# The beginning of a decoder trunk on one core: norm weights ahead of unit 0, later units requested behind its landing, and transposes by diagonal products and by pairs

## The reference, cut to what matters

```python
def rmsnorm(x, g):
    y = xf * lax.rsqrt(jnp.mean(xf * xf, axis=-1, keepdims=True) + EPS)
    return (y * g.astype(jnp.float32)).astype(x.dtype)
...
    a_u, a_v, b_q, b_k, b_v, c_b, c_c, c_x, d_a, d_g = split_cols(h @ w_in)
    y_a = sgu_mixer(a_u, a_v, ...)          # gelu of a_u and a_v first
```

## Time and profile before

| what | value |
|---|---|
| median of 3 runs | 771.77 us (771.01 to 772.01) |
| the profiled execution's own time | 771.82 us |
| its span, first to last instruction | 768.9 us |
| mean granted TensorE clock | 0.999 |
| busy: PE, PEld | 757.4 us (98%), 679.2 us (88%) |
| busy: DVE, ACT, POOL | 637.1 us (83%), 499.6 us (65%), 22.5 us (3%) |
| line 914, DVE, w_lo of a full unit | mean 2195 ns, x140 |
| line 564, ACT, w_hi of a full unit | mean 1841 ns, x140 |
| chain that ended last | PE 95%, DVE 2%, ACT 1%, issue 1%, DMA 1% |

### The profile page before, as it was taken

How to read it: one execution, slowest core, us unless ns; L and a number is a source line. 1 busy time by engine, 2 the same in 40 slices (tenths; PEclk the granted TensorE clock), 3 DMA queues, 4 the chain that set the end, 5 groups by cost and what they waited for, 6 DMA issues and landing times.

```text
span 768.9 us, 12945 instructions
## 1 busy us (share of the span) xinstructions
PE 757.4 (98%) x4794; PEld 679.2 (88%) x4794; DVE 637.1 (83%) x856; ACT 499.6 (65%) x592; POOL 22.5 (3%) x42
## 2 busy tenths in 40 slices
PE   7999999999999999999999999999999999999997
PEld 7899999999878888888799999999988888888885
DVE  5858899469779998989785779956977999898995
ACT  7535566645588877777662547565548978776773
POOL 4030000000000000000001000000000000000000
PEclk9999999999999999999999999999999999999999
DMA  8866345357727999999465553534764599999961
GB/s 306 280 220 218 112 165 165 100 197 253 257 72 270 327 388 347 354 344 333 139 219 166 189 194 113 189 111 139 271 215 170 175 346 356 367 355 331 346 240 55
DMA packets 86418, 180.57 MB, mean 235 GB/s; under 512 B 13238, under 2 KB 25176, under 8 KB 86360
## 3 DMA queue, kind: packets, MB, share of 16 engines
q1 hardware_dynamic: 86360, 179.79, 67.2%
HBM read 178.72 MB, written 1.05 MB: 234 GB/s over the span
## 4 chain that ended last, share of the span: by engine, by line
PE 95%; DVE 2%; ACT 1%; issue 1%; DMA 1%; POOL 0%; DVEq 0%; ACTq 0%; POOLq 0%
PE bank L1507 28%; PE bank L1509 28%; PE bank L1508 28%; PE bank L1913 2%; PE bank L1824 1%; PE bank L1794 1%; PE bank L1939 1%; PE bank L1673 1%; PE bank L1578 1%; DMA x<-in_x 1%; PE bank L1581 0%; PE bank L1787 0%; ACT gates L574 0%; ACT gates L587 0%; PE bank L1908 0%
## 5 line engine op out<-in xcount | busy, mean ns | idle before, releaser
L914 DVE TENSOR_TENSOR w_lo<-raw,w_hi 128x2048 fp32r<-128x2048 f32 (+1 forms) x140 | 304.7, 2195 | 54.8 <-ACT w_hi L564 54.0
L564 ACT ACTIVATE w_hi<-raw 128x2048 fp32r<-128x2048 f32 (+1 forms) x140 | 256.1, 1841 | 127.6 <-PE bank L1509 126.9
L1507 PE MATMUL bank<-a_hi,w_hi 128*128 128x256 f32 x688 | 195.8, 285 | 0.6 <-DVE a_lo L980 0.6
L1509 PE MATMUL bank<-a_lo,w_hi 128*128 128x256 f32 x688 | 194.6, 283 | 0.0
L1508 PE MATMUL bank<-a_hi,w_lo 128*128 128x256 f32 x688 | 194.6, 283 | 0.0
L1507 PE MATMUL bank<-w_hi,y_lo 128*128 128x512 f32 x408 | 161.2, 395 | 0.0
L1509 PE MATMUL bank<-w_lo,y_lo 128*128 128x512 f32 x408 | 159.2, 390 | 0.0
L1507 PEld LDWEIGHTS bank<-a_hi,w_hi 128*128 128x128 f32 x688 | 131.9, 192 | 1.6 <-issue 1.5
L1508 PEld LDWEIGHTS bank<-a_hi,w_lo 128*128 128x128 f32 x688 | 132.0, 192 | 0.1
L1509 PEld LDWEIGHTS bank<-a_lo,w_hi 128*128 128x128 f32 x688 | 132.0, 192 | 0.0
L1508 PE MATMUL bank<-w_hi,y_hi 128*128 128x512 f32 x272 | 106.1, 390 | 0.0
(11 more groups left out here) (334 smaller groups left out, 960.8 us busy)
## 6 DMA issues: line engine op xcount, KB each, us to landing
raw<-in_w_gate SPq DMA_DIRECT2D x56, 512.0 KB, 4.6
raw<-in_w_e_gate SPq DMA_DIRECT2D x42, 512.0 KB, 4.5
raw<-in_w_e_up SPq DMA_DIRECT2D x42, 512.0 KB, 6.1
mid<-in_w_e_down SPq DMA_DIRECT2D x36, 512.0 KB, 5.9
raw<-in_w_in SPq DMA_DIRECT2D x32, 512.0 KB, 6.2
raw<-in_w_e_gate SPq DMA_DIRECT2D x40, 256.0 KB, 4.6
raw<-in_w_e_up SPq DMA_DIRECT2D x40, 256.0 KB, 5.6
mid<-in_w_e_down SPq DMA_DIRECT2D x40, 256.0 KB, 5.4
```

The lines of the kernel that those rows point to most:

```text
L564: a.activation(w_hi[:, at.part(n), 0:w], raw_at(slot)[:, 0:w], ACT.Copy).then_inc(hi_done, at.count(n))
L914: v.tensor_tensor(w_lo[:, part, 0:w], raw_at(slot)[:, 0:w], w_hi[:, part, 0:w].bitcast(F32), ALU.subtract).then_inc(split_done, at.count(n))
L1507: mm(ps, a2[0], b2[0], start=first, stop=False, skip_group_check=shared)
L1509: return mm(ps, a2[0], b2[1], start=False, stop=last, skip_group_check=shared)
```

## The change

- SyncE issues the norm weights of layer 0 ahead of unit 0. Behind unit 0 it waits until both its DMAs have landed, and only then requests units 1 to 3 and all that stands behind them.
- Layer 0, half 0: DVE copies x unscaled into tile order when it has landed, and scales the identity matrix by the row factors (a diagonal matrix). TensorE multiplies each tile by the diagonal, which transposes and scales at once. Half 1: DVE scales all eight tiles, ScalarE none; TensorE transposes them as before.
- Layer 0: h_hi of k = 0 and 1 is made by DVE, directly ahead of their h_lo, instead of by ScalarE, whose high part of unit 0 no longer stands behind a scaling. The semaphore of h_hi is raised by 3 at k = 2 to make up for them.
- `keep_warm` goes from 14 to 11 products ahead of the transposes and from 6 to 4 behind, in layer 0.
- Layer 1: TensorE waits for both scaled halves and then transposes by pairs: tiles k and k + 4 of both halves (four transposes), then the signal for that pair. Before, half 1's transposes gave the signals.

```diff
+            norm_gains(0)
             load(At(0, 0, False), 0, *units_a[0], 0)
-            norm_gains(0)
+            sp.wait_ge(landed[0], 16 * DMAS)
             first_units(At(0, 0, False), 0, 1)
...
-            scale_part(0)
             hi(At(0, 0, False), 0)
...
-                for k in range(KT):
+                for k in range(0 if l else 2, KT):
...
+                if l == 0:
+                    dve.wait_ge(pool_consts, 3)
+                    dve.wait_ge(x_loaded[0], 16)
+                    v.tensor_copy(xn[:, 0, :, :], x[:, 0, :].rearrange("q (p c) -> q c p", c=KT)).then_inc(S("n1_x"), 1)
+                    mean_square_in(0)
+                    dve.wait_ge(S("n1_rs"), 1)
+                    v.tensor_scalar(diag[:, 0, :], ident[:, :], rs1[:, 0:1], None, ALU.mult).then_inc(S("n1_d"), 1)
+                    mean_square_in(1)
+                    scaled(1, 0)
...
+                    if l == 0 and k < 2:
+                        dve.wait_ge(par_g, 16)
+                        dve.wait_ge(S("n1_t"), k + 1)
+                        v.tensor_scalar(h_hi[:, k, :], bank[4 + k][:, 0:256], g1[:, k:k + 1], None,
+                                        ALU.mult).then_inc(S("h_hi_first"), 1)
+                        dve.wait_ge(S("h_hi_first"), k + 1)
...
-                keep_warm(4, 16 if l else 14)
...
+                keep_warm(4, 16 if l else 11)
...
+                    for k in range(KT):
+                        mm(turned_at(0, k), xn[:, 0, k, :], diag[:, 0, :], start=True, stop=True, skip_group_check=True)
+                    pe.wait_ge(S("n1_x"), T)
+                    for k in range(4):
+                        tp(turned_at(1, k), xn[:, 1, k, :], ident[:, :])
+                        tp(turned_at(1, k + 4), xn[:, 1, k + 4, :], ident[:, :]).then_inc(S("n1_t"), 1)
+                    keep_warm(3, 4)
+                else:
+                    pe.wait_ge(S("n1_x"), T * (l + 1))
+                    pe.wait_ge(S("n1_xa"), l)
+                    for k in range(4):
+                        for kk in (k, k + 4):
+                            for t in range(T):
+                                last = tp(turned_at(t, kk), xn[:, t, kk, :], ident[:, :])
+                        last.then_inc(S("n1_t"), 1)
```

## The result

The changed kernel takes 773.73 us (median of 15 executions, 770.85 to 777.34), the kernel before beside it 771.62 us (median of 15, 770.51 to 772.99). The ratio is 1.0029, with a 95% interval of 1.0018 to 1.0041: slower by 0.3%. The forecast was 771.9 with a range up to 773.6, and "the same" as the likeliest case.

A forecast was written before the change was run, and what follows sets the result against it. TensorE alone was taken to bound nearly everything after the first product. The 1.75 us front gain was eaten by later requests (0.2 us slower), layer 1 cost 0: span 769.1, time 771.9 us, range 769.9 to 773.6.

The forecast's parts named there:

- the compute chain: Layer 0, ahead of the first weight product: it starts 1.75 us earlier, at 11.25 to 11.4 instead of 13.10.
- a bound of 1.3: Layer 0's diagonal products: hidden at the fast pace, cost 0; at 0.213 us each they delay half 1 by 1.3 us.
- Landings: SyncE's queue at the start: unit 0 landed at 8.95, unit 1 at 14.3, unit 3 at 19.8 instead of 16.9.
- my own sign (8.8 to 9.1): Unit 0's landing: the forecast would be wrong if it came at another time than 8.8 to 9.1.
- layer 1: Layer 1's transposes by pairs: cost 0, from -0.1 to +0.3 us.
- The delay d: SyncE's request of unit 4: 2.9 us later, at 24.6 for 21.67; 0.7 to 5.6 possible.
- case B: SyncE regains its holding in issuing: d 0.7 to 2.6, front gain partly or wholly through, 770.0 to 770.8; chance 0.28.
- case A: The forecast: landings pace SyncE, d 2.6 to 3.3, net 0.15 us faster to 0.6 slower, 771.6 to 772.4; chance 0.5.
- The limit that I summed at: TensorE at unit 4, 2.74 us in hand: net gain the smaller of 1.75 and 2.74 - d, giving -0.2 us.
- The stall: TensorE waiting for layer 0's mixer parameters: landed near 24, TensorE there at 22.9, about 1 us.
- The step that failed: From the mixer parameters to unit 4: about 1 us of waiting counted at its length, not adding to the next limit.
- the base: Time around the span: 2.9 us, from one profiled execution of 771.82 us with span 768.9.

The follow-up runs named there:

- the repeat: The changed kernel run again with no edit, on one chip with other kernels: 775.0 us, ratio 1.0045.
- the first trace: The first profiled execution of the changed kernel, no edit: 771.44 us, span 769.7.
- without pairs: The changed kernel with layer 1's transposes in the order of before: 775.79 us, ratio 1.0051.
- with warm-up in the stall: The changed kernel with eight unused warm-up products ahead of TensorE's wait for the layer 0 mixer parameters: 772.47 us, ratio 1.001.
- with the parameters early: The changed kernel with the 14 mixer parameter requests ahead of unit 3's: 776.48 us, ratio 1.0062.
- pairs alone: The kernel before with only layer 1's transposes by pairs: 772.28 us, ratio 1.001.
- new front, old requests, with pairs: The changed kernel with the request order of before, run in two groups: 770.25 us, ratio 0.9969, and 769.87 us, ratio 0.9977.
- new front, gains ahead, no wait of SyncE: The changed kernel without the wait on unit 0's landing, norm weights still ahead of unit 0: 770.44 us, ratio 0.9983.
- new front, old requests, no pairs: The changed kernel with requests and layer 1 transposes as before, leaving layer 0's compute chain: 771.04 us, ratio 0.9987.
- late parameters, warm-up in the stall: Layer 0's new compute chain, old requests but router's ahead of mixer's, plus 22 unused warm-up products before the parameter wait: 775.28 us, ratio 1.0047.
- requests alone: The kernel before with only the new request order and SyncE's wait for unit 0: 772.23 us, ratio 1.0006.
- late parameters: Layer 0's new compute chain with old requests, but five router requests ahead of the 14 mixer ones: 778.18 us, ratio 1.0085.
- the third set: Last experiments: changed kernel unedited, with old requests, without SyncE's wait, and late parameters with warm-up: 775.0, 769.87, 770.44, 775.28 us.
- the clean pair: Late parameters without and with 22 unused warm-up products in TensorE's idle stretch: 778.18 and 775.28 us; profiled spans 775.4 and 772.4.

## Why the prediction was wrong, point by point

**Right: the compute chain.** First product forecast at 11.25 to 11.4, found at 11.27. Second root forecast at 0.55 us, found 0.55: the 1.39 us were DVE's scaling beside it, not GpSimd's own. The Trainium skill ("SBUF — State Buffer", section "Who interferes with whom") says that a VectorE operation can hold the pair of ports that it shares with GpSimd for its whole length; the two durations agree. The diagonal products took 2.49 us, not 1.8, and ended at 9.75 rather than by 9.2 to 9.5. Half 1 was ready at 9.17, but its transposes started at 9.59; in the repeat, where the diagonal products took 2.10 us, they started at 9.23. So that cost some 0.35 us here, where I had taken 0 of a bound of 1.3. In the other traces with this request order the first product came at 11.34 to 11.66, behind a later unit 0.

**Landings: right in the first trace, early for the others.** Unit 0 landed by 8.89 (forecast 8.95), unit 3 at 19.8 (19.8). But ScalarE could begin on unit 0 only at 9.38, 9.45, 9.59 and 9.70 in the traces without pairs, of the repeat, with warm-up in the stall and with the parameters early, all with this request order up to there. By my own sign (8.8 to 9.1) the forecast was wrong in these four. I had given the earlier norm weights 0.0 to 0.3 us; 0.6 to 0.9 is what these four show. SyncE's wait hands that on whole and a little more: the last parameter went out at 20.64, 20.96 and 20.95 in the first three of these, at 20.04 in the first trace. The estimate from the Trainium skill's fit of a DMA ("DMA: Bandwidth & Descriptors", section "Anatomy of one DMA — SWDGE (gpsimd) path") was 18.3: too early by 1.5 us on this queue.

**Right: layer 1.** Forecast 0, found 0.07 us shorter.

**The delay d: near in size, its mechanism not shown.** Forecast 2.9 us at unit 4. Found 2.2 in the first trace, which lies in case B's range, and 3.1, 3.7 and 2.7 in those without pairs, of the repeat and with warm-up. SyncE was again held on sgb (1.54 us) and now on snk (1.39). The second hold ended at 18.08, between the landings of unit 2 (17.10) and unit 3 (19.80), so case A's pacing by landings is not borne out by it.

**The limit that I summed at did not bind.** I worked out -0.2 us at unit 4. With 2.74 us in hand there TensorE did not wait at unit 4 in any trace of the changed kernel. The net gain was set at the parameters: in the first trace 1.83 less 1.11 of idling and 0.2 that do not read as idle, 0.52 us at unit 4. The stall was forecast at "about 1 us" and is 1.11 in this trace, 1.75 and 2.33 in two others. The 1.11 are luck in part: the last request went out 0.9 us before the 20.96 that d = 2.9 gives, and needed 3.95 us to land, where I had put 2.5 "or somewhat more" and allowed 3.0. In the repeat it went out at 20.96 and needed 4.43. So the term was too small by 0.9 to 1.4 us, and that the sum lies near the spans at full clock is luck too.

**The step that failed** is the one that put the stall at its own length: "about 1 us of stall. It does not add to the next". From it I went on to the next limit as if TensorE behind the stall were the TensorE before it. In two of the four traces with a stall of 1.1 to 2.3 us it is not: the clock falls to 0.50 while the dense products of unit 2 run, and 3.4 and 6.8 us there cost 1.6 and 3.2. I had weighed the clock at one place only, in the diagonal products, where I took the fast pace because the transposes of before ran fast after an idle stretch. That row was read rightly for its place, and it was no evidence for this one. The forecast had no case for it, and therefore no price.

**How the sum stands.** At full clock an execution of the changed kernel has a span of 769.1 to 769.5, where I had 769.1. Beyond that, here is what the stall adds, as mean span above the span at full clock:

| kernel | TensorE at the parameters | mean above full clock |
|---|---|---|
| before (three groups) | no wait | 0.8, 0.9, 1.3 |
| pairs alone | no wait | 1.5 |
| new front, old requests, with pairs (two groups) | no wait | 0.6, 0.7 |
| new front, gains ahead, no wait of SyncE | no wait | 1.2 |
| new front, old requests, no pairs | no wait | 1.6 |
| changed, warm-up in the stall | covered | 1.3 |
| late parameters, warm-up in the stall | covered | 0.9 |
| requests alone | idle 1.3 | 1.5 |
| changed without pairs (5 executions) | idle 1.8 | 3.3 |
| changed (two groups) | idle 1.1, 2.3 | 2.7, 3.9 |
| late parameters | idle 5.3 | 4.1 |

(The idle times are those of the profiled executions. The second group of the changed kernel has no execution at full clock and takes the first's 769.3 as its base, the last row that of the same kernel with warm-up, 772.4.) Every kernel with no wait or a covered one is 0.6 to 1.6 us above its span at full clock on the mean; in their traces the lapses lie in the router's stage or later. With the new front and the stall uncovered it is 2.7 to 4.1. The requests alone stay within the spread of the kernels without a wait: their slowest execution, shown above, lost time at the stall, and none of the other twelve has as low a mean clock. Part of the changed kernel's excess is the stall itself, which was 1.2 us longer in its second trace. The kernel with the parameters early is not in the table: it has no execution at full clock, and its wait is at unit 4. The result, +2.44 us of mean span against before's first group, is then 0.5 at full clock, where I had worked out 0.2, and 1.9 more in what executions with a longer stall or a fallen clock add. Which of the lapses in it lie behind the stall is not recorded for executions without a trace.

A second, smaller error lies in the base. I took 2.9 us around the span from one profiled execution; over all executions it is 1.9. An execution of before at full clock takes 770.8 on the mean, and its median of 771.6 already has a lapse of its own in it. I had no term for that. With 1.9 my sum would have been 771.0, so this error brought the forecast nearer to the result.

**What stays open.** Why the last parameter was requested at 20.04 in one trace of the changed kernel and at 20.96 in another: unit 0's landing differs by 0.6 us and all requests behind the wait move with it; what moves unit 0 was not tried. Why the clock falls behind one stall and not behind another: it fell behind 1.3, 2.3 and 5.3 us, and behind 3.4 at unit 4, and not behind 1.1 and 1.8, in single profiled executions. Further, why TensorE's clock falls between 217 and 229 us, or between 588 and 598, in nine of the 14 traces and not in the others: four of the nine are of kernels with no stall, so such lapses need no stall. Whether the change makes them more frequent was not tried. And how much of the changed kernel's excess is the clock and how much a longer stall: the warm-up in it gave back 1.1 to 2.3 us of mean span, in another group of runs than the changed kernel's, so this is no split. The table behind the third set splits single traces only. The clean pair, 3.0 us, holds for the kernel with the late parameters.

## What to carry to other kernels

Price a new wait of TensorE twice: by its length, and by what the products behind it cost at the lower clock, which here was 3.2 us behind a wait of 1.3 in one trace, and nothing behind 1.1 and 1.8 in two others. If a short idle stretch ahead of dense products can't be removed, fill it with unused products; that gave back 3.0 us in the clean pair of traces, where the stretch was 5.3 us, and 1.1 to 2.3 us on the mean, between groups of runs, where it was one or two. A wait in a queue that issues requests delays everything queued behind it: here it was put in for unit 0, which needed no help in the old order (the front alone gained 1.6 us at full clock without it), and was paid for by the last of fourteen small parameters. The best version found is the changed kernel with the old request order: ratio 0.9969 (0.9956 to 0.9981) and 0.9977 (0.9966 to 0.9987) in two groups.

## What the runs showed of the hardware

- Behind an idle stretch of 1.3, 2.3, 3.4 or 5.3 us TensorE's granted clock fell to 0.50, at no fixed distance: with 1.3 us of idling ending at 25.93 it fell at 27.0 and came back at 33.9; with 5.3 us ending at 27.84 it had fallen at 27.5, before the work began. After stretches of 1.11 and 1.75 us, in other executions, it did not fall at all. With the 5.3 us filled by unused products it stayed at 1.00.
- The last of fourteen small requests (4 KB) landed 3.95 us after its issue in the first trace, and 3.5 to 4.4 in four others.
- GpSimd's root of 128x1 took 1.39 us beside DVE's scaling of 128x1024 and 0.55 alone (the first root before, and both in the changed kernel).
- SyncE's issue of a tiny transfer took 1.4 to 2.0 us while large transfers were outstanding: on sgb and snk in the changed kernel, on sgb and conv_b before. Which request it meets is no property of the order alone: in two runs of the same kernel (changed, old request order) snk took 1.63 and 0.43 us and conv_b 0.31 and 1.37.
